# A diffusion backbone layer: two gate tiles moved into the first stage, the rotary key tile summed on VectorE, modulation strips in pairs

## What is computed

```python
sh, sc, gt = split(silu(c) @ w_ada + b_ada)          # the same for c_ctx
h_l = rmsnorm(x) * (1.0 + sc) + sh                   # h_c likewise, 256 tokens
u_l = h_l @ w_in                                     # 4928 columns
u_c = h_c @ w_in[:, OFF_KV:OFF_MLA_G]                # keys and values, rotary key
hy   = hyena_mix(u_l[hyena]) * silu(hyena gate)      # two long convolutions
mla  = attend(queries, keys of both) * silu(gate)    # 8 heads, 768 keys
pool = pool_mix(u_l[pool]) * silu(u_l[pool gate])    # 4 groups of 128 columns
x = x + gt * (concat(hy, mla, pool) @ w_out)
return rmsnorm(x) * final_norm_g
```

## Time and profile before

| | |
|---|---|
| Time, median of 3 runs | 904.67 us (904.37 to 905.96) |
| The profiled execution | 904.4 us, its span 902.6 us |
| PE busy | 886.0 us, 98% |
| DVE, ACT, POOL busy | 693.6, 426.1, 197.9 us |
| PE in the chain that ended last | 86% |
| DMA in the chain | 6%, most of it w_ada |
| PE's granted clock | 0.997 |

### The profile page before, as it was taken

The page is one execution under the profiler, slowest core; times in us unless marked ns, Lnnn a source line. Parts: engine busy times, 40 slices in busy tenths (PEclk is TensorE's granted clock), DMA queues, the critical chain, the costliest instruction groups (busy, mean ns, idle before and its releaser), DMA issues.

```text
span 902.6 us, 12257 instructions
## 1 busy us (share of the span) xinstructions
PE 886.0 (98%) x4754; PEld 738.9 (82%) x4754; DVE 693.6 (77%) x859; ACT 426.1 (47%) x633; POOL 197.9 (22%) x167
## 2 busy tenths in 40 slices
PE   9999999999999999999999999999999999999995
PEld 6777788888888888888888788989898988888884
DVE  5555898789997699967887484778686788878795
ACT  4655567535334444333323332645464547545354
POOL 2222200310003100001003653101000110594551
PEclk9999999999999999999999999999999999999998
DMA  9999933235462453489874463657556335875844
GB/s 365 416 418 423 414 133 111 86 113 209 137 171 101 117 163 135 169 262 330 296 287 171 118 186 99 210 175 162 160 141 152 93 141 197 287 216 193 242 171 186
DMA packets 36885, 184.08 MB, mean 204 GB/s; under 512 B 4411, under 2 KB 5819, under 8 KB 26716
## 3 DMA queue, kind: packets, MB, share of 16 engines
q1 hardware_dynamic: 32528, 147.25, 44.1%
q0 software_dynamic: 3968, 35.65, 16.4%
q10 hardware_dynamic: 332, 0.40, 0.1%
HBM read 177.39 MB, written 37.75 MB: 238 GB/s over the span
## 4 chain that ended last, share of the span: by engine, by line
PE 86%; DMA 6%; DVE 4%; ACT 2%; issue 1%; SPq 0%; POOL 0%; ACTq 0%; DVEq 0%
PE pp L2335 40%; PE pp L2645 17%; PE pp L2365 17%; DMA ada_raw<-in_w_ada_dram 5%; PE pp L2250 3%; PE pp L2226 2%; PE pp L2611 2%; DMA w_raw<-in_wb_dram 1%; PE pp L2602 1%; PE pp L2603 1%; DVE softmax_stats L1853 1%; PE pp L2256 1%; DMA ada_raw<-in_w_scale_dram 1%; DVE pt_lo L1868 1%; ACT U L1140 0%
## 5 line engine op out<-in xcount | busy, mean ns | idle before, releaser
L2335 PE MATMUL pp<-h_hi,w_hi 128*128 128x512 f32 x544 | 213.1, 392 | 1.2 <-ACT U L984 1.2
L2335 PE MATMUL pp<-h_hi,w_lo 128*128 128x512 f32 x544 | 211.9, 389 | 0.0
L2335 PE MATMUL pp<-h_lo,w_hi 128*128 128x512 f32 x544 | 211.8, 389 | 0.0
L1568 DVE TENSOR_TENSOR w_lo<-w_raw,w_hi 128x1024 fp32r<-128x1024 f32 x68 | 91.9, 1352 | 65.1 <-ACT w_hi L931 64.4
L931 ACT ACTIVATE w_hi<-w_raw 128x1024 fp32r<-128x1024 f32 x68 | 71.8, 1056 | 134.8 <-PE pp L2335 110.0
L2335 PEld LDWEIGHTS pp<-h_hi,w_hi 128*128 128x128 f32 x544 | 102.2, 188 | 23.1 <-issue 1.6
L2335 PEld LDWEIGHTS pp<-h_hi,w_lo 128*128 128x128 f32 x544 | 102.1, 188 | 21.5
L2335 PEld LDWEIGHTS pp<-h_lo,w_hi 128*128 128x128 f32 x544 | 102.2, 188 | 20.5
L1899 DVE TENSOR_TENSOR wo_lo<-wo_raw,wo_hi 128x2048 fp32r<-128x2048 f32 x28 | 75.4, 2699 | 18.3 <-ACT wo_hi L1185 18.3
L2645 PE MATMUL pp<-wo_hi,side_hi 128*128 128x512 f32 x224 | 87.3, 390 | 0.0
L2645 PE MATMUL pp<-wo_hi,side_lo 128*128 128x512 f32 x224 | 87.2, 389 | 0.0
(11 more groups left out here) (367 smaller groups left out, 1923.7 us busy)
## 6 DMA issues: line engine op xcount, KB each, us to landing
w_raw<-in_wb_dram SPq DMA_DIRECT2D x68, 512.0 KB, 3.9
ada_raw<-in_w_ada_dram SPq DMA_DIRECT2D x15, 2048.0 KB, 13.2
w_out_sums<-in_w_out_dram POOLq DMA_DIRECT2D x16, 1024.0 KB, 8.3
w_gate_raw<-in_w_gate_dram SPq DMA_DIRECT2D x16, 1024.0 KB, 6.6
wo_raw<-w_out_sums SPq DMA_DIRECT2D x16, 1024.0 KB, 5.0
wo_raw<-in_w_out_dram SPq DMA_DIRECT2D x12, 1024.0 KB, 5.2
wa_raw<-in_wa_dram SPq DMA_DIRECT2D x14, 288.0 KB, 7.9
UG<-in_xT_dram SPq DMA_DIRECT2D x7, 512.0 KB, 8.7
```

The lines of the kernel that those rows point to most:

```text
L1568: eng.tensor_tensor(lane(wb_lo, n % KW), lane(wb_raw, n % KW), lane(wb_hi, n % 2), ALU.subtract).then_inc(wb_lo_done, 1)
L2335: mm = eng.matmul(ps[i][:], w, x, start=(kk == 0 and m == 0), stop=(kk == KT - 1 and m == 2))
```

## The change

`wa` gets two more tiles, the last two of the four pool gate tiles, and the second stage has 16 groups, so its chunks run to 63. Bank 7, bank 5 and banks 0 to 4 and 6 are shared out anew: the rotary key tile has no bank of its own now. In each step PE makes its product with the x tile (part 0) and the context tile (part 1) in bank 7, and DVE adds them into `k_rope` in SBUF (`key_part_added`), after `first_tokens(j + 1)` and `first_context(j + 1)`. PE waits for the addition of part 0 before it writes part 1, and for that of part 1 before bank 7 is used again. Blocks of w_ada are taken in pairs in steps 1, 3, 5, 7, 9, 10 and 12, singly in steps 0 and 14 (`STRIPS`); LATE moves from 13 to 10. Both root sums of the tokens are made in step 11.

The two gate tiles are copied out by ACT early in the second stage, multiplied by `rstd` on POOL, stored to DRAM at slot 3, loaded into their place at slot 57 and finished with a SiLU at chunk 63. Steps of the norms of queries and keys move up by one to four chunks, and the attention weights' loads and splits by four. The pooling uses buffers elsewhere, DVE's `low(0)` waits for its end. The two sum transfers after pooled tiles go into the attention steps. At the end of the kernel the means and roots of row tiles 2 and 3 are made at chunk 26, and each row tile is scaled as soon as it can be. Half of the first scale strip is issued from ACT's queue.

The core of the diff (left out are buffer addresses, semaphore counts, and the shifted chunk numbers):

```diff
-A_TILES = 5
-B_GROUPS = 17
+A_TILES = 7
+A_BANKS = (0, 1, 2, 3, 4, 6)
+B_GROUPS = 16
...
-EARLY, LATE = 2, 13
+EARLY, LATE = 2, 10
...
+STRIPS = {-1: (0,), 0: (1,), 1: (2, 3), 3: (4, 5), 5: (6, 7), 7: (8, 9), 9: (LATE, 11), 10: (12, 13), 12: (14, 15), 14: (16,)}
...
-SUM_SLOTS, SUM_POOLS, SUM_STEPS = (8, 10, 12, 14, 16, 18, 24, 26, 28, 30, 32, 34, 36), (0, 2), (1, 2, 4, 5, 7, 8, 10, 11, 13, 14, 16, 17, 19, 20, 22, 23, 25)
+SUM_SLOTS, SUM_POOLS, SUM_STEPS = (8, 10, 12, 14, 16, 18, 24, 26, 28, 30, 32, 34, 36), (), (1, 2, 4, 5, 7, 8, 10, 11, 13, 14, 16, 17, 19, 20, 21, 22, 23, 25, 26)
...
-                if j == LATE:
-                    load_ada(LATE)
-                load_ada(block_of(j))
+                for b in STRIPS.get(j - 1, ()):
+                    load_ada(b)
...
+                if slot == 3:
+                    eng.wait_ge(a_scaled, 4)
+                    eng.dma_start(gates_out, late_gates[:]).then_inc(gates_kept, 16)
...
-                if slot == 63:
-                    eng.wait_ge(pool_done, 4)
+                if slot == 57:
+                    eng.wait_ge(g_sum, 16)
+                    eng.wait_ge(mirror_done, 4)
+                    eng.wait_ge(gates_kept, 64 + 16)
+                    eng.dma_start(UG[:, 14 * L:16 * L], gates_out).then_inc(gates_back, 16)
+                    eng.wait_ge(kr_done, 1)
                     eng.dma_start(gate_rows_[:], t["b_gate"].to_broadcast([P, D])).then_inc(gate_in[0], 16)
...
-                eng.tensor_tensor(lane(wa_lo, s, 4 * P, AW), raw[:, 0:4 * P], hi[:, 0:4 * P], ALU.subtract)
-                eng.tensor_tensor(hi[:, AW - DR:AW], raw[:, 4 * P:AW - DR], hi[:, 4 * P:AW - DR], ALU.subtract).then_inc(wa_lo_done, 1)
+                eng.tensor_tensor(lane(wa_lo, s, 6 * P, 6 * P), raw[:, 0:6 * P], hi[:, 0:6 * P], ALU.subtract)
+                eng.tensor_tensor(hi[:, AW - DR:AW], raw[:, 6 * P:AW - DR], hi[:, 6 * P:AW - DR], ALU.subtract).then_inc(wa_lo_done, 1)
+            for i in range(2):
+                eng.wait_ge(evA_done, 3 + i)
+                x = late_gates[:, i * L:(i + 1) * L]
+                eng.tensor_tensor(x, x, rstd[:], ALU.mult).then_inc(a_scaled, 1)
...
-                rows_out(block_of(j + 1))
+                if j in STRIPS:
+                    rows_out(j)
                 if j == 0:
                     rows_of_w(1)
-                modulation(j + 1)
+                for b in STRIPS.get(j, ()):
+                    modulation(b)
                 first_tokens(j + 1)
...
+            def late_gate(i):
+                eng.wait_ge(mmA_done, KT + 2)
+                eng.activation(late_gates[:, i * L:(i + 1) * L], ps[2 + i][:], ACT.Copy).then_inc(evA_done, 1)
+            def late_gates_done():
+                eng.wait_ge(gates_back, 64 + 16)
...
+                    eng.activation(ug(14 + i), ug(14 + i), ACT.Silu, bias=shift_cols[:, 2 + i:3 + i], scale=1.0).then_inc(evA_done, 1)
...
+                    last_root(0)
+                    last_root(1)
+            last_scale(0)
             row_squares(0, 2)
             row_squares(1, 2)
-            last_root(0)
-            last_root(1)
+            last_scale(1)
             row_squares(0, 3)
             last_root(2)
-            for i in range(3):
-                last_scale(i)
+            last_scale(2)
             row_squares(1, 3)
             last_root(3)
             last_scale(3)
...
+            def key_part_added(j, part):
+                n = LC if part else L
+                dst, x = k_rope[:, part * L:part * L + n], ps[7][:, 0:n]
+                eng.wait_ge(kr_part, 2 * j + part + 1)
+                if j == 0:
+                    eng.tensor_copy(dst, x).then_inc(kr_added, 1)
+                else:
+                    eng.wait_ge(kr_added, 2 * j + part - 1)
+                    eng.tensor_tensor(dst, x, dst, ALU.add).then_inc(kr_added, 1)
...
-                first_context(j + 1)
+                if j != 11:
+                    key_part_added(j, 0)
+                    first_context(j + 1)
+                    key_part_added(j, 1)
+                else:
+                    first_context(j + 1)
+                    key_part_added(j, 0)
+                    key_part_added(j, 1)
+                    token_reciprocal(0)
+                    token_reciprocal(1)
+                if j + 1 == LATE:
+                    for k in range(EARLY):
+                        shifted(k)
...
-                if j in (10, 11):
-                    token_reciprocal(j - 10)
+                if j + 2 == KT:
+                    key_part_added(KT - 1, 0)
                 if j >= 12:
                     tokens(2 * j - 24)
+                if j + 2 == KT:
+                    key_part_added(KT - 1, 1)
+                if j >= 12:
                     tokens(2 * j - 23)
                 if j >= 11:
                     scale(2 * j - 22)
                     scale(2 * j - 21)
-                if j + 2 == LATE:
-                    for k in range(EARLY):
-                        shifted(k)
             def chunk_low(n):
                 eng.wait_ge(wb_hi_done, n + 1)
...
+                    row_mean(0)
+                    row_mean(1)
                 wo_low(n)
                 if n in (16, 17):
                     side_low(5, n - 16)
                 if n in (22, 23):
                     side_low(3, n - 22)
-            block_out(0, 2)
-            block_out(1, 2)
-            for i in range(3):
-                row_mean(i)
+            for i in range(2):
+                block_out(i, 2)
+                last_blocks(i)
+            row_mean(2)
             block_out(0, 3)
-            for i in range(3):
-                last_blocks(i)
+            last_blocks(2)
             row_mean(3)
             block_out(1, 3)
             last_blocks(3)
...
+            def combine(j):
+                eng.wait_ge(rows_done, sorted(STRIPS).index(j) + 1)
+                for b in STRIPS[j]:
+                    c, r = comb_column(b), 64 * comb_column(b)
+                    if b >= EARLY:
+                        eng.matmul(ps[7][:, c:c + 2], rows[:, r:r + P], comb[:], start=True, stop=True)
+                    eng.matmul(ps[7][:, c + 2:c + 4], rows[:, r + P:r + 2 * P], comb[:], start=True, stop=True).then_inc(comb_mm, 1)
...
+            def key_part_of(j, part):
+                s = j % 2
+                if part:
+                    eng.wait_ge(a_lo_done, 2 * j + 2)
+                    eng.wait_ge(kr_added, 2 * j + 1)
+                w, n = lane(wa_hi, s, AW, AW)[:, AW - P:AW], LC if part else L
+                for m, x in enumerate((c_hi, c_lo) if part else (a_hi, a_lo)):
+                    mm = eng.matmul(ps[7][:, 0:n], w, lane(x, s, n, n), start=m == 0, stop=m == 1)
+                mm.then_inc(kr_part, 1)
...
-                for i in range(A_TILES):
-                    if i == 2 and j:
-                        eng.wait_ge(a_lo_done, 2 * j + 2)
-                    if j == 0 and i == 4:
+                if j == KT - 1:
+                    eng.wait_ge(kr_added, 2 * j)
+                    key_part_of(j, 0)
+                for i in range(6):
+                    if j == 0 and i == 5:
                         eng.wait_ge(mlp_arg, 3)
                     mm = tile(i, j)
-                    if j == 0 and i == 1:
-                        combine(1)
-                        hidden(1)
-                    if i == 0 and j + 1 < KT:
-                        if j in (11, 12):
-                            eng.wait_ge(root_done, j - 10)
-                        ada_vectors(block_of(j + 1))
-                    if j + 2 == LATE and i == 3:
-                        eng.wait_ge(root_done, 2)
-                        ada_vectors(LATE)
-                    if i == 1 and 0 < j < KT - 1:
-                        combine(block_of(j + 1))
-                    if j + 2 == LATE and i == 4:
-                        combine(LATE)
-                    if i == 1 and j in (10, 11):
-                        square_sums(j - 10)
-                    if j == KT - 1 and i < 2:
-                        mm.then_inc(mmA_done, 1)
```

More of the change, by code:

```diff
@@ L341, in backbone @@
         r_kv = U[:, 7 * L:7 * L + LK]
[L342 removed]
+        pads = [at("pool_pads", TMP, 3 * 528)[:, i * 528:(i + 1) * 528] for i in range(3)]
         WQ, WK, WV = (0, 1536), (1536, 2048), (2048, 2560)
@@ L1236, in _ @@
                         centre(i)
+                    for i in range(2):
+                        late_gate(i)
                 if n == 0:
@@ L2265, in shift_columns @@
                 eng.wait_ge(csum_done, KT)
-                eng.wait_ge(root_done, 2)
-                for i in range(8):
-                    w = shift_x[:, i * P:(i + 1) * P] if i < 5 else shift_c[:, (i - 5) * P:(i - 4) * P]
+                eng.wait_ge(kr_added, 2 * KT)
+                for i in range(10):
+                    w = shift_x[:, i * P:(i + 1) * P] if i < 7 else shift_c[:, (i - 7) * P:(i - 6) * P]
```

(34 more changed lines are left out.)

211 lines of the change are left out of this document (107 added, 104 removed).

## The result

The changed kernel takes 913.43 us (median, 912.74 to 914.26), the kernel before 904.81 beside it: 1.0091 times as long, 95% interval 1.0077 to 1.0106. So it is 8.6 us slower, where +4.1 was forecast: the sign was right, but the forecast was half of what came, and 913.43 lies just above the stated range of 901 to 913. The profiled execution took 913.3 us, its span is 911.5 against 902.6.

The account below looks back on a forecast made before the run. PE was taken to bound the kernel, level with DMA in the first stage. Terms +0.9 - 2.1 - 1.2 - 2.1 + 1.9 + 8.0 - 1.3 = +4.1 on 904.4 us gave 908.5, range 901 to 913.

Parts of the forecast that it names:

- The mechanism: First stage: POOL's split collides with DVE's two-input work, so PE waits for the rotary key's additions, 8.0 us.
- VectorE at chunk 3: Early second stage: two POOL products for the moved gate tiles are hidden by PE, 0 us.
- the level steps: First stage, steps 6, 11, 14, 15 and the long ones: additions come out level, taken as 0, at most 3 us together.
- moved tiles, shift columns: 96 matmuls move from second to first stage, -21.9 and +22.4 us, small shift-column matmuls +0.4: together +0.9 us.
- pairs, on PE alone: First stage: 16 strip events become 9, each saving 0.30 us of refilling: -2.1 us.
- waits for w_ada, steps 2, 5, 8, 9: First stage: DMA falls behind PE's need, so four waits for strips of w_ada go: -2.1 us.
- early pair: Step 1: block 3 of w_ada is wanted a step sooner, so PE waits 1.9 us (bounds 0.5 and 2.5).
- waits for the addition: First stage: PE waits for DVE's addition of part 0 in steps 2, 4, 8 and 13: +8.0 us, upper bound 11.
- evacuation near chunk 60: Near the second stage's end: PE's one wait for an ACT evacuation goes as two sum transfers move: -1.2 us.
- end of the kernel: Last stores: tokens 2 and 3 scaled some 4 us sooner, so the span ends sooner: -1.3 us (bounds -0.3 and -2).
- the walk of the step: First stage, short steps: engine timelines put the addition late by 1.2, 1.8, 1.8 and 3.2 us in steps 2, 4, 8, 13.
- Rival 1: First stage: no collision of POOL's split with DVE, 1.1 us of waits instead of 8.0, 901.6 us; chance 0.32.

Follow-up runs that it names:

- b2_sums: The kernel before with only the two w_out sum transfers behind pooled tiles 0 and 2 moved into the attention stage: 903.06 us.
- a1: The changed kernel with GpSimd's split of the next step's weights started only behind VectorE's a_lo in steps 2, 4, 8 and 13: 909.18 us.
- c4: The kernel of a5_singles with part 0 added before a_lo of the next step and the gate products behind the last h_lo: 905.61 us.
- a5_singles: The changed kernel with most strips of w_ada one block at a time again, 14 events instead of 9: 907.47 us.
- a6: The changed kernel with GpSimd's split behind a_lo in four steps, part 0 added before a_lo, gate products behind the last h_lo: 915.96 us.

## Why the prediction was right or wrong

The mechanism came as forecast; what failed are terms put at nothing: VectorE at chunk 3 (+1.5), the level steps (+2.1), step 14 with its fall of TensorE's clock (+1.2) and the start with step 0 (+1.3). Other terms gave a little back.

Term by term (us). Free steps, without a wait, are taken from the runs: 6.70 before, then 8.13 for a single, 10.40 and 5.59 for a long and a short one.

| Term | forecast | measured | from |
|---|---|---|---|
| moved tiles, shift columns | +0.9 | +1.4 | 15 x 1.43 and 2.0 in step 15, and 408.0 - 430.0 |
| pairs, on PE alone | -2.1 | -1.9 | 7 x 0.27 |
| waits for w_ada, steps 2, 5, 8, 9 | -2.1 | -1.7 | before, over 6.70 |
| early pair | +1.9 | +1.6 | step 1, 11.99 - 10.40 |
| waits for the addition | +8.0 | +9.3 | below |
| evacuation near chunk 60 | -1.2 | -1.8 | b2_sums, 431.8 - 430.0 |
| end of the kernel | -1.3 | -1.7 | tail |
| VectorE at chunk 3 | 0 | +1.5 | 409.5 - 408.0 |
| start, and step 0 | 0 | +1.3 | 12.6 - 11.6, and 0.3 |
| step 14 | 0 | +1.2 | 9.31 - 8.13 |
| square sums and roots, steps 10 to 12 | 0 | -0.7 | 0.7 of waits instead of 1.4 |
| third stage | 0 | +0.5 | |
| sum | +4.1 | +9.0 | spans: +8.9 |

- **The mechanism was right, and the walk of the step nearly exact.** It gave steps 2, 4, 8 and 13 late by 1.2, 1.8, 1.8 and 3.2 us; they are late by 1.0, 1.5, 1.5 and, with some of the fall of the clock, 3.2. The collision of POOL's split with DVE's two-input work was the cause of most of it (a1: 4.2 us less without it); in step 13 a wait of 1.0 us stayed, where the prediction without collisions had 1.1. Rival 1 is refuted: POOL did start with DVE's square sums.
- **"Level, I take 0" was too low.** Steps 3, 5, 6, 7, 9 and 10 are 0.15 to 0.38 late each, step 12 0.5: 2.1 us together, of the 3 that I allowed. A balance of 9.0 against 9.0 is as likely late as early, and late costs where early gains nothing; half of the allowance belonged in the sum.
- **Three more terms at nothing are the larger part of the miss:** chunk 3, step 14 and the start, 4.0 us. Chunk 3 is the step that failed most plainly: "two POOL products early in the second stage ... hidden by PE". They are hidden from PE but not from DVE, whose `h_tmp` they hold up for 2 us when it is late already. I had used that very collision in the first stage and looked for "DVE late" only at the second stage's end, where nothing came. Step 14's part is mostly the clock, some 1.0 us, which no term of the forecast had. The start is in part chance, and an early one would have won nothing, since the wait for block 3 takes it up (PE began on that block at 24.7 to 25.1 in all six, and the forecast had it landed at 24.7): the first step began at 11.5 to 11.9 us in the kernel before and its variants, at 11.6 to 12.6 in those of the change.
- **The sum by parts hid what the kernel could have been.** The waits stood under the rotary key, the pairs at -2.1 as a gain. But steps 2, 4, 8 and 13 were short only because of the pairs; with single strips in most steps and the addition first the waits are 1.7 us (c4). The prices of the pairs were right, but which part to blame was not.
- **The Trainium skill's rule on ports** (page "SBUF — State Buffer", section "Who interferes with whom") was used for the reciprocals, and they ran free, in 3.53 us for two, as in the earlier trace rows, with POOL's split inside (a5_singles):

```profile
118.11 3.53 DVE L1526 RECIPROCAL rstd<-h_tmp 128x256 f32<-128x256 f32 x2
...
119.16 1.83 POOL L710 TENSOR_TENSOR wa_lo<-wa_raw,wa_hi 128x768 fp32r<-128x768 f32 x1 [4.40 <-ACT wa_hi L901]
```

  The addition from PSUM, with one SBUF input, ran free too (0.69 beside POOL's split at 53.49, above).
- **The end and the sums** went as forecast, and gained 0.4 and 0.6 us more.

## What to carry to other kernels

Before work is grouped into larger events, walk the shortest step that this leaves against the engine that is loaded in every step: here pairs saved PE 0.3 us each and cost 1.5 in two of the short steps. An edit that is "hidden by PE" must also be held against the next busiest engine, with the collisions that it brings. And walk cures together: an order that is good while a_lo waits for nothing is bad once it waits for PE.

## What the hardware showed beyond that

DVE instructions with one input were not all safe beside POOL. At the end of the changed kernel, POOL's products lie beside DVE's scaling of a block, which takes 0.49 us alone:

```profile
896.42 2.73 POOL L800 TENSOR_TENSOR product<-product,UG 128x512 f32<-128x512 f32 x2 [7.06 <-ACT out_tmp L1232]
...
896.72 1.28 DVE L2011 TENSOR_SCALAR product<-product,row_scale 128x512 f32<-128x512 f32 x1
897.92 1.51 DVE L2015 TENSOR_SCALAR product<-product,row_scale 128x512 f32<-128x512 f32 x1
```

Together 1.8 us lost, off the path here. A reciprocal of half the size, 1.75 us, lost nothing. The same section of the Trainium skill says that `tensor_scalar` can enter a mode that uses both ports and then does contend, and the trace agrees: the operation that runs at 512 elements in 0.49 us is the one that is blocked. In a group of instructions both engines may lose: 2.44 us for a 1.85 us split and 2.94 for 1.48 us of sums, in step 4.

TensorE's clock fell to half for some 3 us near the end of the first stage in eight of the twelve kernels with seven pooled tiles, and in steps 3 and 5 in a ninth (a6), and never in the first two stages of the kernel before or its three variants. In a6 two falls came with waits of 2.2 us, and two other waits of that length had none behind them. The thing to note is the masking: a fall in step 15 and a late VectorE at chunk 3 each cost 1.5 us, and with the first present the second did not show.
